# Hybrid encoder layer on one core: two gate groups kept on chip, layer norm in two wide passes by halves, output projection begun over seven of eight blocks, last tile finished half by half

## What is computed

```python
proj = einsum('bsd,de->bse', x, w_in)            # q, k, v, recurrence inputs, branch gates
attn = sliding_window_gqa_sinks(...)
rec  = hgrn2(...)
mixed = sigmoid(ga) * (attn @ w_proj_attn) + sigmoid(gh) * (rec @ w_proj_hgrn)
x = layer_norm(ALPHA * x + mixed @ w_out, ln1_g, ln1_b)
# PEER, per token t: top 16 of 128 keys twice, top 16 of the sums -> experts e, g = softmax(scores)
hid = einsum('thkd,td->thk', u[e], x);  act = gelu(hid)
ffn = einsum('thk,thkd->td', g * act, v[e])
x = layer_norm(ALPHA * x + ffn, ln2_g, ln2_b)
# layer_norm: (x - mean) * rsqrt(var + 1e-5) * g + b over the 1024 columns
```

## Time and profile before

| | |
|---|---|
| median of 3 runs | 1640.93 us (1637.55 to 1645.9) |
| the profiled execution | 1638.83 us, its span 1636.8 us |
| TensorE busy | 1536.4 us, 94% |
| VectorE busy | 1126.5 us, 69% |
| ScalarE busy | 272.9 us, 17% |
| GpSimd busy | 611.6 us, 37% |
| mean granted TensorE clock | 0.965 |
| moved by DMA | 540.77 MB, mean 330 GB/s |

### The profile page before, as it was taken

The page is one execution under the profiler, slowest core; times in us unless marked ns, Lnnn a source line. Parts: engine busy times, 40 slices in busy tenths (PEclk is TensorE's granted clock), DMA queues, the critical chain, the costliest instruction groups (busy, mean ns, idle before and its releaser), DMA issues.

```text
span 1636.8 us, 17961 instructions
## 1 busy us (share of the span) xinstructions
PE 1536.4 (94%) x6542; PEld 1093.9 (67%) x6542; DVE 1126.5 (69%) x2364; ACT 272.9 (17%) x543; POOL 611.6 (37%) x516
## 2 busy tenths in 40 slices
PE   7798998789998799999999999999789999999997
PEld 7697777565557566788889999998534444444443
DVE  1414799987769999999967889898644534444443
ACT  2601213621010111111123333432000000000000
POOL 0000543466667473322324555556533323232100
PEclk9899998879999799999999999999899999999999
DMA  7586967777999797898888999999999999999962
GB/s 289 209 276 215 399 225 267 255 244 265 413 405 372 270 409 284 313 328 301 316 289 298 413 412 414 411 385 397 404 400 371 381 383 375 391 379 386 365 206 103
DMA packets 146663, 540.77 MB, mean 330 GB/s; under 512 B 14992, under 2 KB 34192, under 8 KB 134032
## 3 DMA queue, kind: packets, MB, share of 16 engines
q0 software_dynamic: 73728, 268.47, 43.8%
q1 hardware_dynamic: 71696, 254.38, 41.6%
q10 hardware_dynamic: 1152, 16.78, 2.4%
HBM read 508.11 MB, written 31.46 MB: 330 GB/s over the span
## 4 chain that ended last, share of the span: by engine, by line
PE 76%; DVE 12%; DMA 6%; issue 3%; ACT 2%; SPq 1%; POOL 0%; DVEq 0%
PE bank L834 26%; PE bank L859 25%; PE bank L739 7%; PE bank L814 6%; PE bank L852 3%; DVE arena L1160 2%; DMA arena<-v_cols_d 2%; DVE arena L1175 2%; PE bank L774 2%; PE bank L749 1%; DMA arena<-gates_d 1%; PE bank L751 1%; PE bank L586 1%; DMA arena<-w_items_d 1%; DMA arena<-u_d,arena 1%
## 5 line engine op out<-in xcount | busy, mean ns | idle before, releaser
L1589 POOL DMA_INDIRECT arena<-u_d,arena x256 | 334.2, 1305 | 501.8 <-DVE arena L1160 254.5
L859 PE MATMUL bank<-arena 128*128 128x512 f32 x1024 | 444.5, 597 | 17.4 <-DVE arena L1498 12.1
L834 PE MATMUL bank<-arena 128*128 128x256 f32 x2048 | 453.8, 381 | 3.6 <-DMA arena<-u_cols_d 3.6
L1589 POOL DMA_INDIRECT arena<-v_d,arena x256 | 277.2, 1083 | 419.3 <-DVE arena L1175 357.2
L834 PEld LDWEIGHTS bank<-arena 128*128 128x128 f32 x2048 | 386.2, 191 | 53.6 <-issue 3.8
L859 PEld LDWEIGHTS bank<-arena 128*128 128x128 f32 x1024 | 196.1, 192 | 265.4 <-issue 245.1
L1175 DVE SCALAR_TENSOR_TENSOR arena<-arena 128x1024 f32<-128x1024 f32 x256 | 327.6, 1280 | 11.0 <-DMA arena<-v_d,arena 3.0
L1160 DVE CUSTOM_DVE_ANT_0 arena<-arena 128x1024 f32<-128x1024 f32 x256 | 304.3, 1220 | 30.5 <-DMA arena<-u_d,arena 29.7
L1498 DVE TENSOR_TENSOR arena<-arena 128x256 f32<-128x256 f32 x128 | 53.2, 419 | 216.6 <-DMA arena<-act_d 177.7
L814 PE MATMUL bank<-arena 128*128 128x128 f32 (+1 forms) x512 | 118.1, 392 | 1.4 <-ACT arena L1020 1.4
L739 PE MATMUL bank<-arena 128*128 128x128 f32 (+1 forms) x512 | 113.8, 384 | 0.2 <-DMA arena<-w_items_d 0.2
(11 more groups left out here) (199 smaller groups left out, 1072.9 us busy)
## 6 DMA issues: line engine op xcount, KB each, us to landing
arena<-w_items_d SPq DMA_DIRECT2D x66, 1024.0 KB, 7.3
arena<-u_cols_d SPq DMA_DIRECT2D x128, 512.0 KB, 7.0
arena<-v_cols_d SPq DMA_DIRECT2D x128, 512.0 KB, 7.3
gates_d<-arena ACTq DMA_DIRECT2D x8, 2048.0 KB, 11.9
arena<-gates_d SPq DMA_DIRECT2D x16, 1024.0 KB, 11.2
act_d<-arena SPq DMA_DIRECT2D x12, 1024.0 KB, 9.3
arena<-act_d SPq DMA_DIRECT2D x12, 1024.0 KB, 13.0
arena<-u_d,arena POOLq DMA_INDIRECT x256, 8.9
```

The lines of the kernel that those rows point to most:

```text
L834: last = mm(bank[:, 4 + c % 2, 0:ND], u_buf[:, c % UBUFS, k, :], B.act_in[:, k, B.n - ND:B.n], start=k == 0, stop=k == KC - 1)
L859: last = mm(bank[:, 2 * n + half, :], act_slot(i)[:, n * P:(n + 1) * P], v_buf[i % VBUFS][:, half * 512:(half + 1) * 512], start=i == 0, s ...
L1589: pool.indirect_dma_start(rows[:, r % SLOTS, :], None, table, bass.IndirectOffsetOnAxis(eidx[:, t, k:k + 1], 0)).then_inc(landed[r % SLOTS ...
```

## The change

**Gates.** Groups 6 and 7 stay in the two stage buffers; six groups are stored and read back (768 KB instead of 1 MB a load, pieces of 1 KB as before). `weigh` multiplies 192 columns by the loaded and 64 by the kept gates. The quads are spread over chunks 53 to 115 instead of 56 to 113, with 104 instead of 96 rows between them; MID_ROWS stays.
**v blocks.** Eight buffers instead of six: two in the space of the finished routing, two in that of the one-hots (after the last quad), four in that of the u buffers (each after one of the last four hidden chunks). The second gate load now comes behind all eight.
**Output projection.** Two units of front A, four of front B sum seven blocks as soon as the seventh block is mixed, and the eighth when that is there. Rows around it: 148 before the first unit and two more before each of the next six, 160 in all, where it was 152, 161 and 170.
**Layer norm.** Statistics of each half as soon as it is there; then (x - mean) * g in one pass while ScalarE takes the root; then * rstd + b in two halves, each with its own signal; TensorE transposes after each half. All six norms use it.
**The end.** The last four blocks are summed by tile and half (four groups), VectorE follows by halves, and each half tile is stored by itself.

```diff
-UBUFS, VBUFS = 4, 6
+UBUFS, VBUFS = 4, 8
+STORED = GROUPS - 2
-SPREAD_AT, SPREAD_END = 56, 114
+SPREAD_AT, SPREAD_END = 53, 116
-HOT_ROWS = 96
+HOT_ROWS = 104
-ODD_STEP, AT_OUT, OUT_STEP, HGRN_STEP, STATE_STEP = 5, 152, 9, 3, 2
+ODD_STEP, AT_OUT, OUT_STEP, HGRN_STEP, STATE_STEP = 5, 148, 2, 3, 2
...
-        v_buf = [view(kb, D) for kb in (140, 144, 64, 68, 72, 76)]
+        v_buf = [view(kb, D) for kb in (172, 176, 164, 168, 48, 52, 56, 60)]
...
-            sp.wait_ge(idx_ready, 2 * PH)
+            sp.wait_ge(pick_ready, len(DENSE))
             for i in range(2):
                 load_v(i)
             for k in range(2):
-                sp.wait_ge(g_stored[k], 16 * (GROUPS // 2))
+                sp.wait_ge(g_stored[k], 16 * (STORED // 2))
             load_gates(0)
-            for i in range(2, VBUFS):
+            sp.wait_ge(g_done, QUADS)
+            for i in range(2, 4):
+                load_v(i)
+            for i in range(4, VBUFS):
+                sp.wait_ge(h_done, EXPERTS + i + 1 - VBUFS)
                 load_v(i)
             load_gates(1)
...
+                begun = 2 if nt == 1 else 4
+                pe.wait_ge(F.mix_out, KC - 1)
+                for u in range(begun):
+                    item_in(pe, F, I_OUT + out_units(F)[u][0])
+                    for c in range(KC - 1):
+                        sum_out(u, c)
                 pe.wait_ge(F.mix_out, KC)
                 for u, (k, t) in enumerate(out_units(F)):
                     item_in(pe, F, I_OUT + k)
                     if u >= 4:
                         pe.wait_ge(F.y_out, u - 3)
-                    for c in range(KC):
+                    for c in range(KC - 1 if u < begun else 0, KC):
+                        last = sum_out(u, c)
                     last.then_inc(F.y_done, 1)
...
             def combine_last():
+                for n in range(len(DENSE)):
+                    for half in range(2):
+                        for i in range(EXPERTS - LAST, EXPERTS):
...
+                            last = sums(i, n, half)
+                        last.then_inc(o_done, 1)
...
-                if k == GROUP // QUAD - 1:
+                if k == GROUP // QUAD - 1 and g < STORED:
                     act.wait_ge(g_out, q + 1)
                     nc.scalar.dma_start(gates_d[g], stage[g % 2].rearrange("p e t -> p (e t)")).then_inc(g_stored[g % 2], 16)
...
-                    if t == 0 and k < N_OUT - 1:
-                        rows_until(AT_OUT + OUT_STEP * k)
+                    rows_until(AT_OUT + OUT_STEP * min(u, F.nt * (N_OUT - 2)))
...
+                    if k >= N_OUT - 2:
+                        dve.wait_ge(F.y_out, u + 1)
+                        half_stats(F.x1[:, t, :], k - (N_OUT - 2))
...
+            def norm_scale(t, y, std_ready, ready):
+                steps(lambda: v.scalar_tensor_tensor(out=y, in0=y, scalar=mv[:, 0:1], in1=ln_gb[:, 0, :],
+                                                     op0=ALU.subtract, op1=ALU.mult))
                 dve.wait_ge(std_ready, t + 1)
                 steps(lambda: v.reciprocal(rstd[:, :], rstd[:, :]))
-                steps(lambda: v.tensor_scalar(dst, src, mv[:, 0:1], rstd[:, 0:1], ALU.subtract, ALU.mult))
-                steps(lambda: v.tensor_tensor(dst, dst, ln_gb[:, 0, :], ALU.mult))
-                v.tensor_tensor(dst, dst, ln_gb[:, 1, :], ALU.add).then_inc(ready, 1)
+                for half in range(2):
+                    part = slice(512 * half, 512 * half + 512)
+                    v.scalar_tensor_tensor(out=y[:, part], in0=y[:, part], scalar=rstd[:, 0:1], in1=ln_gb[:, 1, part],
+                                           op0=ALU.mult, op1=ALU.add).then_inc(ready, 1)
...
-                v.tensor_tensor(a, a, g_buf[b % 2][:, :, i % GBLK, :], ALU.mult).then_inc(w_ready, 1)
+                v.tensor_tensor(a[:, 0:STORED, :], a[:, 0:STORED, :], g_buf[b % 2][:, :, i % GBLK, :], ALU.mult)
+                v.tensor_tensor(a[:, STORED:GROUPS, :], a[:, STORED:GROUPS, :], g_kept[:, :, chunk(i), :],
+                                ALU.mult).then_inc(w_ready, 1)
```

98 lines of the change are left out of this document (50 added, 48 removed).

## The result

| | before | changed |
|---|---|---|
| median of 6 runs each, same chip | 1643.41 us (1637.55 to 1649.31) | 1626.05 us (1616.92 to 1628.27) |
| ratio, 95% interval | | 0.9898 [0.9874, 0.9922] |
| profiled execution, its span | 1638.83, 1636.8 | 1628.27, 1626.5 |
| TensorE idle before the picks, seam, v waits | 0, 12.06, 5.28 | 10.32, 8.80, 0 |

The changed kernel is 1.0% faster. The forecast was 1617, with a range of 1603 to 1629. The range holds the time, but the likeliest value is 9 us too fast.

A forecast was written before the change was run, and what follows sets the result against it. TensorE, at 94% of the span, was taken as the bound, with VectorE a hidden second bound before the picks. Front 6.8, seam 13.1 and tail 2.5 sum to 22.4 off 1638.83: 1616.4, given as 1617 us, range 1603 to 1629.

The forecast's parts named there:

- The tail: After TensorE's last matmul: VectorE's remaining work by halves takes 4.85 us instead of 7.33, a gain of 2.5.
- the v waits: Combine stage: with eight v buffers the waits for v go, 5.3 us, and their 1.8 of clock.
- front B: Output projection and norm of front B: query projection begins 15.6 us earlier, VectorE is only 1.0 ahead.
- VectorE as the hidden second bound: Picks, chunk 52: VectorE's routing comes late, TensorE waits 7.4 us and pays 3.0 of clock; 6.8 of the front remain.
- The third rival: Chunks 50 to 52: VectorE is not the bound and the whole 17.2 us survives, giving 1607; chance 0.08.
- Front A: Output projection and layer norm of front A: early start loses 0.7 us, the norm gains, net 1.6 for both engines.
- The seam: Between hidden and combine: gates land 6.0 us after the last hidden matmul, gain 6.0; with the v waits 13.1.
- The step that failed: From query projection A to the mixing end of B: no difference between the kernels, 0 us.
- The slower rival: Spreading stage: one-hots come late behind rows, TensorE waits at each quad, giving 1647 us; chance 0.05.
- The fifth rival: Combine stage: gains are handed to new waits for v or gates, within 8 us of before, 1635; chance 0.07.
- The first rival: Seam does not clear, gates land as late as before; 3 to 9 us less gain, 1623 to 1627; chance 0.16.
- the prediction's own signs of being wrong: Wrong if chunk 52 comes over 12 or under 6 us earlier, or the seam keeps 10 us or none.

The follow-up runs named there:

- late_picks: Changed kernel with exponentials, pick transposes and spreading three chunks later (53, 55, 56 to 118); 1617.98 us, ratio 0.9849 to the kernel before.
- rest_only: Changed kernel with projection, rows and first norm of the fronts as before; 1638.93 us, ratio 0.9928 to the kernel before.
- gates_wide: Changed kernel with gates laid out so a load is one 6 KB piece a partition instead of six of 1 KB; 1623.37 us, ratio 0.9892 to before.
- after_again: Changed kernel, unedited, profiled and timed once more; 1626.43 us against 1650.62 for the kernel before, ratio 0.9864.
- before_again: Kernel before, unedited, profiled and timed once more; 1653.25 us, ratio 1.0009 to the kernel before.
- front_only: Kernel before with only the edits of the fronts (begun units, rows around them, first norm by halves); 1644.65 us, ratio 0.995 to before.
- gather_held: Changed kernel with GpSimd running 4 rows ahead instead of 12 for its first 24 gathers; 1629.02 us, ratio 0.9925 to before.
- the second comparison: Changed kernel, unedited, timed again against the kernel before on the chip of the first four experiments; 1626.43 against 1650.62 us, ratio 0.9864.
- gates_early: Changed kernel with the first gate load issued within the u loads, after that of chunk 118; 1619.32 us, ratio 0.9862 to the kernel before.
- early_held: Changed kernel with later picks and spreading, earlier first gate load, and GpSimd 4 rows ahead for its first 24 gathers; 1621.95 us, ratio 0.986 to before.

## Why the prediction was right, and where it missed

**The tail, the v waits, front B** were right in mechanism and size. The tail is 4.84, predicted 4.85. The v waits are gone, and combine is 7.7 shorter for 7.1 forecast. The query projection is 17.3 earlier after the mixing end, predicted 15.6. The last norm ends 46.9 after the mixing (552.06), where my stepping of the twelve units gave 48.8: the units ran in one piece, and the stepping of VectorE between them was too slow by two. The clock after the wait costs 3.2, predicted 3.0.

**VectorE as the hidden second bound** was right, and is the step on which the forecast turned. The third rival (all 17.2 survive, 1607) fell: TensorE waited 10.32 before the picks, predicted 7.4. VectorE was 0.5 ahead of its old place instead of 1.0, TensorE was further ahead. late_picks shows that the 11.8 behind it can be had.

**Front A** gave 2.6 instead of 1.6. The norm's part was right (3.96 against 3.9). Of the two waits for weights that I stepped, unit 1's 0.8 did not come: three units run in one piece of 10.53. The other did, and its item was there at 128.02 instead of 129.2, so that the last matmul ends at 131.74 and not at 132.7. That is the 1.0.

**The seam** is where a term was mis-sized: 3.3 instead of 6.0. Of the 2.7, 0.9 are a slip in the sum: before, the load landed 11.1 after the last hidden matmul and the idle time was 12.06, so a landing at 6.0 is worth 5.1 and not 6.0. The term had two parts. By its size alone I put the load's landing at 8.1 after the last hidden matmul, and it was used 8.3 after (1176.54 against 1168.28), which is worth the 3.0 I gave it. The other 3.0 were for the rows' queue running dry while the gates are in flight. VectorE did pass row 390 about as early as stepped, 6.6 before the last hidden matmul instead of 6.0 behind it, and the gates came no sooner for it. rest_only passes it only 4.3 before the last hidden matmul and uses its gates 8.3 after it as well. gates_wide shows what the load's length does go by: as many bytes in a sixth of the pieces took 6.1 less. The Trainium skill (DMA: Bandwidth & Descriptors, Queues, rings and completion order) says that the engines take turns between queues by packet, a packet being several descriptors; by that rule larger pieces carry more bytes a turn, and the 13.8 against 19.9 agree. No view here shows the turns themselves.

**The step that failed** is a term that the prediction put at nothing without a reason. It was made against one profiled execution without starvation, and I took its first 500 us as given, apart from front A: 0 for the row where the profiles differ by -12.1. Every later profile with the gather at full rate shows issue waits in A:

| execution | issue waits, 150 to 200 us | query projection A | to the attention matmuls (L655) | to mixing end B |
|---|---|---|---|---|
| before | 0.0 | 34.9 | 187.0 | 354.8 |
| after_again | 3.9 | 43.8 | 188.1 | 363.5 |
| rest_only | 4.8 | 43.9 | 187.2 | 361.5 |
| changed | 7.8 | 50.9 | 192.5 | 366.8 |
| before_again | 8.9 | 50.8 | 193.1 | 366.5 |
| front_only | 9.7 | 50.2 | 192.7 | 368.3 |
| gather_held | 0.0 | 35.2 | 194.4 | 367.7 |

All columns are us; the last three count from the start of query projection A (L655 in the kernel before, L665 in the changed one). The six other kernels with the gather at full rate have 6.4 to 9.8 in the first column, and 364.9 to 367.1 in the last. The end of the query projection, in the timelines of TensorE before and changed:

```profile
175.75 41.45 PE L574 MATMUL bank<-arena 128*128 128x384 f32 x128
```
```profile
189.28 41.45 PE L584 MATMUL bank<-arena 128*128 128x384 f32 x128
```

The table says more than that A starves. The changed kernel loses 16.1 in the query projection, waits and low clock together, but most of it is made up: before, TensorE had waits of 5.1, 2.9 and 2.7 for ScalarE that now are 0, 0 and 1.4. At the attention matmuls 5.5 are left, and 0.2 in rest_only. The other 6.5 come behind them, and they come in all thirteen other profiles, the held ones too: 173.3 to 175.5 from there to the mixing end, where the first profile of before has 167.8. Up to 4.5 of it is one wait about 340 us, here among the waits of TensorE in the changed kernel (140 to 500 us) and before (138 to 500):

```profile
PE bank L686 <- ACT arena L1011: 4.1, 1, 4.1
```
```profile
PE bank L676 <- ACT arena L990: 0.6, 1, 0.6
```

It is 2.0 to 5.0 in the thirteen. ScalarE in turn waits there for something of which the trace has no record. So of the 12.1 starvation in A accounts for 5.5 at most, and the larger part comes behind it, from a cause that is open.

The value, 1617, was 9 too fast for two reasons: the profiled 1638.83 is 4.6 under the median of six executions of its kernel, and the gain was 17.4 and not 22.4. In the second comparison the gain is 24.2 by medians and 22.4 by the ratio. The intervals of the two ratios overlap, so the difference between them needs no cause. That executions of one kernel differ by ten us because starvation is drawn anew each time is argued and not shown: only one execution of a run has a profile. The range, not the value, took the miss up.

One of the prediction's own signs of being wrong did come by its letter: chunk 52 starts at 846.27, 1.6 later than before and not 6 to 12 earlier. Counted from the mixing end, behind the row of -12.1, it starts 8.0 earlier.

**The slower rival** (one-hots late in the spreading stage) did not happen. The busy time by stretch, changed kernel:

```profile
850.00:1168.00 318.00, 318.00 (x1720) 286.62 (x1719) 270.18 (x383) 100.68 (x143) 178.23 (x126) 1.00 0.98 379
```

TensorE is busy through all of it at full clock, at a DMA share of 0.98. The fifth rival was wrong too: combine has no new wait. The first rival (the seam does not clear) comes nearest for that term, with 3 us of gain there, and the load's place in the queue is its mechanism: gates_early gave the rest back. That its 1623 to 1627 holds the measured 1626 is luck: the seam gave 2.7 of the 9 us, and by its own words (3 us less) it should have said 1620.

**Open.** Why the first profiled execution of before was spared, in A and at 340 us. What ScalarE waits for at 340 us. And whether anything other than the gather's rate, the order of its first twelve rows for one, would take the starvation away without the new wait; it was not tried.

## What to carry to other kernels

When the engine with the most busy time is brought forward, ask who hands it its next input and price that engine's own debt; the gain stops there, and a constant that says when the hand-over happens may be worth much: here three chunks gave 11.8 us up to the last hidden matmul. Compare stage by stage against at least two executions of the kernel before: a stretch of one execution may be the lucky one. When waits go from one place, look for them further on before you call them gone. Where a load is late on full DMA queues, count its pieces before its bytes.

## What the runs showed of the hardware

TensorE can stand still for nothing that the profile shows while the DMA engines move data at their full rate. In the query projections the signs are "issue" waits of up to 1.8 us each, a third to two thirds of the usual count of instructions (41 where there were 113, 86 where there were 140), a granted clock that falls with them (0.66 to 0.73 on average), and a DMA share of 1.02 to 1.03 at 410 to 414 GB/s. Single waits of 3.5 to 7.0 us come elsewhere (gather_held, early_held, after_again). At a share of 0.77 and 0.81 they are gone from that place in A. The full share is not enough for them: the first profile of before in A, the changed kernel's in B, and the stretch of the hidden stage in the earlier trace rows run at 1.02 and do not starve. The page's list of DMA queues for the changed kernel has an instruction queue:

```profile
q8 instruction: 52, 0.85, 0.2%
```

That is 0.85 MB / 52 = 16 KB a packet, fetched by the same engines. The Trainium skill (Runtime: NRT & Kernel Launch, Instruction fetch mechanics) says that an engine's instruction memory is refilled in blocks of 16 KiB and that crossing from block to block is mostly hidden. The packet size agrees. That a late refill makes the waits would be the obvious mechanism, and it is not shown. The view of DMA from 160 to 192 us of the changed kernel, which holds all ten waits, lists no packet of that queue, and TensorE works on without a wait where one stands, between 156 and 160 us. What the waits are for, and what decides between two executions of one kernel at the same share, no run here shows.

The size of the pieces sets how long a load takes beside a gather: 768 KB in pieces of 1 KB are used 19.2 to 20.7 us after the issue in six profiles, in pieces of 6 KB 13.8 us after it in one.
